# Conditioning in 2048-feature rows, gated attention with one level per width, function tables loaded ahead

## The reference

```python
# first block
mod = silu(c) @ w_ada + b_ada          # 6144 features, for c and for c_ctx
h   = x * (1 + mod[1]) + mod[0]        # both streams
...                                    # h @ w_in; conv, state-space scan in 2 directions; pooling; gates; w_out
x   = layer_norm(ALPHA * x + mod[2] * y)
...                                    # routed experts (2 of 32 for each token), layer norm
# second block, for l in (0, 1)
mod = silu(c_2) @ ada_w[l] + ada_b[l]  # 9216 features, for c_2 and c_ctx_2
x   = post_norm(x, g1 * swiglu(...))   # feed-forward
...                                    # l = 0: gated linear attention + latent attention; l = 1: neighbourhood attention
x   = post_norm(x, g3 * swiglu(...))
# gated linear attention, forward direction; backward is the flipped one without its diagonal
S_t = diag(a_t) S_{t-1} + k_t^T v_t ;  o_t = q_t S_t
```

## Time and profile before

| | |
|---|---|
| median of 3 runs | 3228.05 us (3225.89 to 3233.68) |
| the profiled execution | 3229.13 us, of it span 3227.3 us |
| PE busy | 2996.7 us, 93% |
| DVE, ACT, POOL busy | 1345.4, 1063.0, 239.0 us |
| moved by DMA | 537.4 MB, 167 GB/s in the mean |

### The profile page before, as it was taken

The page is one execution under the profiler, slowest core; times in us unless marked ns, Lnnn a source line. Parts: engine busy times, 40 slices in busy tenths (PEclk is TensorE's granted clock), DMA queues, the critical chain, the costliest instruction groups (busy, mean ns, idle before and its releaser), DMA issues.

```text
span 3227.3 us, 45764 instructions
## 1 busy us (share of the span) xinstructions
PE 2996.7 (93%) x19958; PEld 2336.7 (72%) x19958; DVE 1345.4 (42%) x1983; ACT 1063.0 (33%) x1565; POOL 239.0 (7%) x275
## 2 busy tenths in 40 slices
PE   6988899889999989999997888999999999898998
PEld 4866699845555548888676646888868887795898
DVE  4655555532222233333476354333343333425554
ACT  4443355322222233222442233322242222425443
POOL 0014470110000000000004000000000000200000
PEclk9988899989999989999898999999989999999999
DMA  7556756399999953232249321323222332420463
GB/s 234 157 182 225 249 161 183 116 383 392 394 390 390 394 191 111 85 105 72 87 134 298 101 79 53 100 83 105 75 95 85 98 100 83 144 92 14 137 187 95
DMA packets 415174, 537.40 MB, mean 167 GB/s; under 512 B 14293, under 2 KB 389877, under 8 KB 390261
## 3 DMA queue, kind: packets, MB, share of 16 engines
q1 hardware_dynamic: 414964, 534.38, 48.6%
HBM read 533.30 MB, written 1.05 MB: 166 GB/s over the span
## 4 chain that ended last, share of the span: by engine, by line
PE 84%; DVE 7%; ACT 4%; DMA 3%; issue 2%; POOL 0%; DVEq 0%; SPq 0%; ACTq 0%; POOLq 0%
PE ps L189 81%; PE ps L188 2%; DVE ar L244 2%; ACT ar L314 1%; DVE LR L244 1%; DMA RAW<-in_ada_w 1%; ACT HR L314 1%; DMA RAW<-in_w_ada 1%; DMA RAW<-in_w_in 1%; PE ps L195 1%; DVE ar L260 1%; ACT arf1i L314 1%; DVE ar L254 1%; ACT L314 1%; DVE X L244 0%
## 5 line engine op out<-in xcount | busy, mean ns | idle before, releaser
L189 PE MATMUL ps<-AH,HR 128*128 128x512 f32 (+1 forms) x2488 | 875.6, 352 | 38.4 <-DVE AL L244 17.6
L189 PE MATMUL ps<-AL,HR 128*128 128x512 f32 (+1 forms) x2488 | 866.8, 348 | 0.0
L189 PE MATMUL ps<-AH,LR 128*128 128x512 f32 (+1 forms) x2488 | 866.1, 348 | 0.0
L244 DVE TENSOR_TENSOR LR<-RAW,HR 128x2048 fp32r<-128x2048 f32 (+3 forms) x232 | 486.1, 2097 | 598.6 <-ACT HR L314 592.1
L314 ACT ACTIVATE HR<-RAW 128x2048 fp32r<-128x2048 f32 (+3 forms) x232 | 404.5, 1745 | 710.8 <-PE ps L189 631.7
L189 PEld LDWEIGHTS ps<-AH,HR 128*128 128x128 f32 x2488 | 476.9, 192 | 109.1 <-ACT ar L314 18.2
L189 PEld LDWEIGHTS ps<-AH,LR 128*128 128x128 f32 x2488 | 476.8, 192 | 58.9
L189 PEld LDWEIGHTS ps<-AL,HR 128*128 128x128 f32 x2488 | 477.2, 192 | 57.1
L244 POOL TENSOR_TENSOR ar<-ar 128x384 f32<-128x384 f32 (+5 forms) x138 | 149.8, 1093 | 1295.4 <-DMA ar<-in_cst 1023.3
L189 PE MATMUL ps<-ar 64*128 64x128 f32 (+9 forms) x1238 | 191.5, 371 | 42.2 <-DVE ar L244 20.4
L189 PEld LDWEIGHTS ps<-ar 64*128 64x128 f32 (+3 forms) x1238 | 119.1, 192 | 103.7 <-issue 37.1
(11 more groups left out here) (203 smaller groups left out, 3679.7 us busy)
## 6 DMA issues: line engine op xcount, KB each, us to landing
RAW<-in_ada_w SPq DMA_DIRECT2D x72, 1024.0 KB, 6.4
RAW<-in_f1i SPq DMA_DIRECT2D x44, 1024.0 KB, 5.1
RAW<-in_f2i SPq DMA_DIRECT2D x44, 1024.0 KB, 5.1
RAW<-in_w_in SPq DMA_DIRECT2D x32, 1024.0 KB, 5.6
RAW<-in_w_ada SPq DMA_DIRECT2D x24, 1024.0 KB, 8.4
RAW<-in_w_eu SPq DMA_DIRECT2D x17, 1024.0 KB, 9.8
HF<-in_w_ed SPq DMA_DIRECT2D x17, 1024.0 KB, 8.9
LF<-in_w_eu SPq DMA_DIRECT2D x17, 1024.0 KB, 10.1
```

What stands on the lines that cost most here:

```text
L189: return self.e.matmul(o, w, x, start=start, stop=stop)
L244: return self.e.tensor_tensor(o, a, b, op) if self.e else NOTHING
```

## The change

1. A chunk is now up to 16 tiles (2048 features) by one block of 128 input rows (`Chunk`): 1 MB in rows of 8 KB. Eight chunks add up in bank 0, which PE keeps for that (`T.lo = 1`, the other banks rotate over 1 to 7), in 4 matmuls of 512 columns each. ACT copies, PE turns and DVE adds only after the last chunk of a part. Numbers of chunks and bytes are the same.
2. `first` has a ring of its own, eight slots in the storage of HR, LR and AL: all its chunks are issued at once. X comes in four transfers behind them, and all of `first` is done before h1, where DVE now makes the context half and ACT the latent half. `dt` has no chunk any more, DVE and ACT cut block 3 in the midst of the softplus.
3. One level for each width: with the halves of both directions in one pair of tensors (`F`, three buffers), 7 levels instead of 14, 32 products of 64 x 64 weights and 64 columns into two banks, masks of 64 columns. The last level (w = 64) is copied by ACT. Still `T.step(2)` for a level, so 14 chunks lie there; the other 15 go to the rounds of `latent_pe`.
4. `ready(f)`: a one-element activation of function f put ahead of a wait, so that the table is loaded there: before each norm, before the norms of the heads, before the rotation.

```diff
-            b, held = T.bank("row", c)
-        for k in range(4):
-            for q in range(4):
-                f = k + 4 * (q % 2)
-                r = T.mm(b[32 * q:32 * q + 32, 0:128], K.CS[:, f, :], w[:, f, q // 2 * 128:q // 2 * 128 + 128], k == 0,
-                         k == 3)
+            b, held = T.hold(0, "row", x.part)
+        for k in range(x.kt):
+            for q in range(4):
+                r = T.mm(b[32 * q:32 * q + 32, 0:n], K.CS[:, x.k + k, :], w[:, k, q * n:(q + 1) * n], x.k + k == 0,
+                         x.k + k == 7)
...
+        for m in range(n):
+            r = T.mm(turned[:, :, m, :], K.mrow[:, 128 * m:128 * m + 128],
+                     K.ident[:, :].rearrange("p (q c) -> p q c", q=4)[:, :, 0:4], True, True)
...
-    D.load(NSLOT)
-    D.dma(K.X[:, :, 256:512], K.dram["xT"].rearrange("(k p) n -> p k n", p=128)).then_inc(K.loaded["x"], 16)
+    D.enter("first")
+    D.load(len(D.ring.plan))
+    D.enter("main")
+    D.load(1)
...
+    def ready(self, f):
+        self.act(self.K.eps[:, 3:4], self.K.eps[:, 0:1], f).then_inc(*self.K.act())
...
-        for tp in range(2):
-            bs = [bank("att", n, p, tp) for p in range(2)]
+        bs = [bank("att", n, p) for p in range(2)]
+        for x in range(8):
+            tt, ft = x // 2, x % 2
+            for half in range(2):
+                ks, qs = tt * 128 + 64 * half, tt * 128 + 64 * (1 - half if n == 6 else half)
+                for p, b in enumerate(bs):
+                    h = slice(64 * p, 64 * p + 64)
+                    r = T.mm(b[64 * half:64 * half + 64, 64 * x:64 * x + 64], k[h, ft, ks:ks + 64],
+                             q[h, ft, qs:qs + 64], True, True)
-    for n, (lv, d) in enumerate(o.levels):
-        T.wait_ge(*dve.of("kq", n))
-        T.wait_ge(*pool.of("kq", n))
-        pairs(n, o.KQ[n % 2], o.KQ[n % 2])
+    for n in range(7):
+        T.wait_ge(*dve.of("kf", n))
+        T.wait_ge(*pool.of("qf", n))
+        pairs(n, o.F[n % 3][:, 0], o.F[n % 3][:, 1])
         T.step(2)
```

390 lines of the change are left out of this document (231 added, 159 removed).

## The result

The changed kernel takes 3185.01 us (median of 4 runs, 3184.89 to 3186.22), the kernel before on the same chip 3230.57 (4 runs, 3225.89 to 3233.68): a ratio of 0.9869, with an interval of 0.9853 to 0.9884. It is 1.3% faster, as forecast in sign, but 27 us above the 3158 predicted. The profiled execution spans 3183.0 us, against 3227.3 before.

A forecast was written before the change was run, and what follows sets the result against it. PE, 84% of the chain that ended last, was taken as the main bound, with DMA at the start. Terms 10 + 3 + 12 + 3 + 2 + 53 - 18 + 5 = 70 us gave 3158; 8-in-10 range 3133 to 3187.

The forecast's parts named there:

- The start: Up to the convolutions: eight chunks issued at once land by 26.3, dt's sum at 47.3, block 5 at 75.9; gain 10 us.
- A chunk on PE: Convolutions and scan: a chunk takes 0.88 us, with its turn 1.04 for 1.33; gains 3 and 12 us.
- The end of the scan: PE's wait of 3.97 us for ACT's copy goes, as no exponents are behind the last copy; gain 3 us.
- The levels: Gated attention's levels: 5.8 us a width, no engine standing out, next projection at 1743 for 1796.5; gain 53 us.
- three subtractions and one product of double size, 5 x 0.737: Levels: DVE's main work per width, which with two masked copies of 0.742 makes 5.2 us.
- Holding bank 0 costs nothing: Scan: a round took four banks of six and now takes two of five, so keeping bank 0 costs nothing.
- What I feared first: Levels: the price of PE's 64 x 64 products, 64 instructions taken at 3.0 us a width, between 2.0 and 4.1.
- Latent attention: Its rounds: 15 chunks and two turns cost 16 us, the late weight cut 4, Exp's table gives back 1.3; loss 18.
- The tables: Norms: loading tables ahead saves 0.6 to 0.8 us in each of seven of eight norms; gain 5 us.
- rival 1: Transfers: the rate stays with three slots in flight, not row length, a chunk stays at 3.5 us; 3174 us, 12%.
- Rival 2: Levels stay bound by handovers, POOL slowed beside DVE, 13 us more; latent attention loses 10 more; 3181 us, 15%.
- the states: The six states: a chunk and its turn cheaper by 0.3 us in each; gain 2 us.

The follow-up runs named there:

- warm: The changed kernel with idle PE products in three waits: behind the scan, ahead of the projection after the levels, ahead of latent attention; 3178.5 us, ratio 0.9842.
- comb3: The changed kernel with y before the scan-end weight cut, three chunks ahead of the levels, the last width's two moved ahead of latent attention; 3182.9 us, 0.9859.
- comb5: comb3 plus idle PE products in its waits, the norms and the scan's groups, and POOL's part of the levels done by DVE; 3144.07 us, 0.9747.

## Why the prediction was right or wrong

**The start: right in its steps.** The eighth chunk's matmuls begin at 25.13 (by 28, forecast), dt's sum reaches DVE at 46.79 (47.3), the fifth block starts at 76.7 (75.9; a gain of 9.4 for 10). PE in after at the first and the last of these:

```profile
25.13 1.93 PE L186 MATMUL ps<-ALF,CS 128*32 128x512 f32 x8 [0.95 <-DMA ALF<-in_w_ada]
...
76.70 0.76 PE L186 MATMUL ps<-AH,HR 128*128 128x512 f32 x1 [5.88 <-DVE LR L241]
```

Then 1 us was lost in the convolution stage where 3 were to be gained: at 198.1 the gain is 8.4. From the fifth block on after has 7.6 us at 1.2 GHz there, before 3.4, which costs some 2 us at most; the rest is open.

**A chunk on PE: the estimate was 0.12 low.** With 512 columns it takes 0.99 us from start to start (1719.62 to 1720.61), and in the form of 256 columns at the end of the scan 1.00 (366.51 to 367.51), not 0.88. That is what it took before, so that what fell is the turn alone. The rounds became 2.86 us all the same (2.9 forecast), since POOL, busy 2.75 of them and idle 0.16, took over as the bound: the sum was right for a reason that it named only as a limit.

```profile
353.02 1.43 POOL L241 TENSOR_TENSOR X<-X,ar 128x256 f32<-128x256 f32 x2 [0.16 <-ACT X L311]
354.40 1.32 POOL L241 TENSOR_TENSOR ar<-ar 128x384 f32<-128x384 f32 x1
355.88 1.42 POOL L241 TENSOR_TENSOR X<-X,ar 128x256 f32<-128x256 f32 x2 [0.16 <-ACT X L311]
```

**The end of the scan: the step failed.** "The last copy is now one round later and no exponents are behind it: 3 us." The stall went from ACT to DVE, whose `y` stood behind two cuts, and grew from 3.97 to 7.23. I asked where the stall goes on ACT, and not what is late next. With `y` first it is 4.39.

**Behind the scan: no step.** The output projection lost 4.6 us, though its instructions are the same. After the wait of 7.23 PE's products of 256 columns stand 0.21 us apart until 381, and 0.12 from there: the first 5 us of the projection ran at 1.2 GHz, and 3.4 us more near 460, where before had none. So a wait can be paid twice, though filling this one (warm) did not win the time back. From the scan's end to the first feed-forward after has some 17 us more at 1.2 GHz than before (0.96 over 815.4 us for 0.97 over 807.5), which could account for the 7.8 us lost (8.5 at most).

**The levels: the term was mis-sized, 45 for 53.** The step that failed is "three subtractions and one product of double size, 5 x 0.737", 3.7 us. That row was measured while POOL was idle for more than half of the time; with POOL beside it the four take 4.5 to 4.9 us in four widths and 6.16 behind the first, and the stage became DVE's: 38.1 us with no chunk at all. Of the 8.5 us by which the levels' 51.1 exceed the forecast's 42.6, 4.9 lie in the six widths, and 4.2 of these in the first. There DVE's late differences hold up ACT's exponentials, and PE's chunk waits 4.33 us for the copy behind them. "Holding bank 0 costs nothing" had been reasoned for the scan only; without chunks that width takes 7.3 us for 10.0. The other 3.6 lie behind the last width: 11.4 us from its start to the projection, for 3.0 + 4.8, since the weights land behind the last chunks. comb3 and comb5, with no chunk in the last width, show 6.2 and 5.9. What I feared first was cheaper than assumed: the 64 instructions of 64 x 64 take 1.09 us from start to start at the full clock and 1.92 at the low one, for 3.0.

**Latent attention: right, 21.9 for 18.** Its 15 chunks cost 1.00 us each and the turns 1.07, some 17 in all; the waits for the cut that were estimated at 4 are there, 1.93, 1.05 and 2.41 us at 1891.59, 1895.94 and 1898.94, minus what the table gave back. Low clock, at 1828 to 1842 and 1896 to 1906, where before it was at 1888 to 1898 only, adds the rest.

**The tables: failed, 0.5 for 5.** "0.6 us is all that is uncovered" was right for the root, whose wait went as the row said. But the sum took the load moved ahead for free: in three norms it delays ACT's copy of the mean by some 1 us, and the clock took part of the rest.

**The transfers: right, and rival 1 fell.** The chunks of the start come 2.49 us apart, 1.049 MB in each, 421 GB/s. In the levels, where three slots are refilled in turn, a stretch in which nearly all of PE's waits are for DMA shows 0.98 and 375 GB/s:

```profile
1700.00:1711.00 11.00, 7.22 (x168) 2.72 (x160) 11.00 (x13) 3.86 (x4) 5.97 (x4) 0.91 0.98 375
```

It is the rows, not the number of slots, that held the rate at 299 GB/s before. By the rule weighed in the prediction (the Trainium skill, "DMA: Bandwidth & Descriptors", section Specifications), rows of 1 KB had been long enough; this case's rows contradict it.

**Rival 2 came nearest, with the time of 3181, but by another way.** It put 13 us to POOL slowed by DVE in the levels and 10 to latent attention. In the run it is DVE that is slowed, the levels fell short by 8 us in all, and latent attention lost 4 more than forecast.

**What the sum left out.** It was made of durations at the clock that before had. "At the low clock a round gives back more" is the only place that speaks of it, and as a gain. Behind the start after has some 17 us more at 1.2 GHz than before, in a span that is 44 shorter: 15 less in the scan, 17 more from there to the first feed-forward, 14 more in latent attention's rounds. That this is because less work of PE now lies between waits is my reading and not shown. Beside this stand some 8 us of gain that came from addresses and that no step had; without them the miss would be some 35 us and not 27, so that the forecast came as near as it did by luck. By the table the largest parts of the miss are the levels (8.0) and the stretch behind the scan (7.8), then the start (4.6), latent attention (3.9) and the states (3.5). The clock lies within these, with 8.5 us at most in the balance of all stages; how much of each it makes wasn't measured.

## What to carry to other kernels

Read the granted clock of each stage before you sum: where PE stands waiting again and again, a removed wait may be repaid in clock. Idle products in the waits are a cheap test of that, but they must be read stage by stage: the same filling gave one kernel 3.6 us in a stage and cost the other 7.8. Price an operation of DVE from rows in which POOL does what it will do in the changed kernel, and try the stage with POOL idle before you split work between them. Follow what a wait held up: the levels' first width was late by a copy on ACT that stood behind DVE's work. Where a stage moves that the change doesn't touch, count instructions in a stretch without waits in both traces: if these differ at the full clock, try addresses, as the change's own worth may be another number.
